# Routing by mask and prefix scan, and a gather inside every preceding expert, in a two-block network with 16 experts

## The chip, the cores and the metric

The kernel runs on one core of one Trainium2 chip. The metric is the device time of one execution in microseconds (us). Before the change it is 2507.76 us, the median of three runs (2507.17 to 2512.72).

## What is computed

Two blocks, one after the other, on 256 tokens of width 1024 (with 16 meta tokens ahead in the first block: T = 272). The first block is a convolution branch and a bidirectional state-space scan, merged, projected and added to the residual h; then comes the part that the change touches:

```python
def expert_choice_ffn(xn, w_router, w_gate, w_up, w_down):
    cap = CAPACITY_FACTOR * T // N_EXPERTS          # 34
    aff = softmax(einsum('btd,de->bte', xn, w_router), axis=-1)
    top_aff, top_idx = top_k(swapaxes(aff, 1, 2), cap)
    xg = xn[bi, top_idx]
    hg = einsum('becd,edf->becf', xg, w_gate)
    hu = einsum('becd,edf->becf', xg, w_up)
    y = einsum('becf,efd->becd', silu(hg) * hu, w_down)
    y = y * top_aff[..., None]
    return zeros_like(xn).at[bi, top_idx].add(y)
```

xn is rms_norm(h). Each of 16 experts picks its own 34 tokens, runs a gated FFN of width 2048 on them, and adds the result back, weighted by the affinity. All is float32. The order of the 34 tokens within an expert doesn't matter to the sum. The second block (gated linear attention, window attention, a product-key layer) follows and isn't touched.

## The kernel before

**Layout.** h lies transposed: 1024 features as 8 tiles of 128 partitions, tokens along the free axis. Each engine has its own written program per stage; semaphores order them.

**End of the mixer.** TensorE computes the eight output tiles with `proj` (line 586), and after tile m calls `norm_sums(m - 2)` (line 767): for three groups of tokens, the sums of squares (weights `s.conf`, one moving column) and the router's products (weights `s.h`, 16 moving columns), each float32 matmul being two records of the trace. The sums of the last three tiles stand behind the last projection. DVE adds the residual (line 579), ACT squares (line 954). SP meanwhile issues the first expert weights (lines 319 to 340).

**Expert weights.** Each expert has 12 units of 2 MB: eight of gate and up rows in turn, four of down. A ring of six slots takes them; the first three units of expert 0 go to rooms of their own (`first_rooms`) that are not filled again. SP (lines 1049 to 1054) waits for unit i to be used and then issues the load six units on. So nine units are loaded before the routing ends.

**Routing** (`experts`, line 1004). ACT and DVE make softmax affinities; TensorE turns the tokens from features-major to tokens-major (line 1127; `s.h` against diagonal matrices of the norm's gain), all six halves, and then the affinities (line 1132) to 16 rows of 272. ACT scales the turned tokens by the norm and rounds them (`tok_hi`, line 1191); DVE makes the rest (`tok_lo`, line 1206). DVE finds the top 34 of each row in five rounds of MAX8, FIND_INDEX8 and MATCH_REPLACE8 (lines 1240 to 1243). From the index lists a spread matrix is made (line 1245), a matmul with ones repeats it over the partitions (line 1140), and a comparison with the row number gives the 0/1 matrix `onehot` for all slots (line 1212). TensorE gathers for eight experts at once, features by slots, as `tok_hi` and `tok_lo` times `onehot` (line 1079, 272 moving columns), ACT copies them out (`picked`, line 1169). `gather(1)` for experts 8 to 15 runs between expert 0 and expert 1.

**An expert.** POOL copies its 34 columns to `tokens` (line 1059). TensorE does 64 products with the tokens as weights (line 1091: 128x34 weights, 512 moving columns, two column groups of the array in turn); ACT silu (1176), DVE the product (1269), and then for each half of the hidden width: four transposes (1099), a DVE copy (1273), 16 down products (1108). ACT copies y (1179); TensorE scatters: eight matmuls of y with `spread` (1118), each added to h by DVE (1277), over two PSUM banks. `spread` (34 rows in each half of the partitions, 272 tokens, the affinity where the token is the slot's) is one DVE instruction per expert from `list_t` (1263), made at the end of the expert before.

What sets the order of TensorE, cut to the loop of an expert:

```python
def expert(e):
    pe.wait_ge(picked, e + 1)
    for u in range(8): ...            # products, L1091
    for c in range(2):
        pe.wait_ge(hidden, 2 * e + c + 1 + FIRST)
        ...                           # four transposes, L1099
        pe.wait_ge(turned_out, 2 * e + c + 1)
        ...                           # down products, L1108
    pe.wait_ge(y_out, e + 1)
    pe.wait_ge(onehot, e + 1)
    for m in range(KT): ...           # scatter, L1118
```

Of the kernel before, what the change touches and what calls it, by code (L numbers as in the profile page):

```python
# [15 lines left out]
P = 128  # L16
# [7 lines left out]
D = 1024  # L24
# [28 lines left out]
FIRST = 1  # L53
# [169 lines left out]
def mixer(nc, s):  # L223
# [60 lines left out]
    with nc.Block() as block:  # L284
# [23 lines left out]
        def _(sp):  # L308
# [5 lines left out]
            for i in range(len(w.units)):  # L314
# [6 lines left out]
                if i in before:  # L321

                    sp.wait_ge(pair_done, PAIRS)
                    s.load_expert_unit(sp, 0, AHEAD + before[i])
# [5 lines left out]
            for u in range(AHEAD - 1):  # L330
                for part in range(2):
                    s.load_expert_unit(sp, 0, u, part)
            s.load_expert_unit(sp, 0, AHEAD - 1, 0)
            s.load_expert_unit(sp, 0, AHEAD)
            sp.wait_ge(tiled, pos["out", 3] + 1)
            s.load_expert_unit(sp, 0, AHEAD + 4)
            sp.wait_ge(tiled, pos["out", 7] + 1)
            s.load_expert_unit(sp, 0, AHEAD - 1, 1)
            s.load_expert_unit(sp, 0, AHEAD + 1)
            s.load_expert_unit(sp, 0, AHEAD + 5)  # L340
# [244 lines left out]
        def _(pe):  # L585
            def proj(t):
# [19 lines left out]
                else:  # L606
# [5 lines left out]
                    for n in parts_of[t]:  # L612
# [8 lines left out]
                        last.then_inc(hi_used, 1)  # L621
                        pe.wait_ge(w_lo, n + 1)
# [144 lines left out]
            def norm_sums(m):  # L767
                pe.wait_ge(hsq, m + 1)
                if m == 0:
                    pe.wait_ge(ystd, 1)  # L770
                    pe.wait_ge(router, 1)

                for j, (t0, n) in enumerate(TT):
                    pe.matmul(ps[0:n, 7, j:j + 1], s.conf[:, m, t0:t0 + n], s.ones[:, 0:1], start=m == 0 and j == 0,
                              stop=False, skip_group_check=True)
                for j, (t0, n) in enumerate(TT):
                    pe.matmul(ps[0:n, 7, EXPERTS * (j + 1):EXPERTS * (j + 2)], s.h[:, m, t0:t0 + n], s.w_router[:, m, :],
                              start=False, stop=m == KT - 1, skip_group_check=True)
# [186 lines left out]
SMALL_ROOMS = 1056  # L965
UNITS = 12


def expert_place(e, u):

    q = (u + EXPERT_RING - AHEAD) % EXPERT_RING
    return q, UNITS // EXPERT_RING * e + (u - AHEAD) // EXPERT_RING + 1


def expert_rows(s, e, u):

    if isinstance(e, int) and UNITS * e + u < AHEAD:
        return s.first_rows[u]
    q = expert_place(0, u)[0]
# [4 lines left out]
def expert_loader(s):  # L984
# [8 lines left out]
    def load(sp, e, u, part=None):  # L993
        if UNITS * e + u < AHEAD:
            sp.dma_start(s.first_rows[u][part], source(e, u)[:, part, :]).then_inc(s.first_in[u], 16)
# [8 lines left out]
def experts(nc, s):  # L1004
# [6 lines left out]
    names = ("rstd3", "std3", "shifted", "exp", "aff", "turned", "lists", "lists_t", "index_rows", "onehot", "tok", "tok_zero",  # L1011
             "tok_out", "tok_rest", "gathered", "gathered_out", "cleared")
    (rstd3, std3, shifted, exped, aff_ready, turned_aff, lists, lists_t, index_rows, onehot_ready, tok, tok_zero,
     tok_out, tok_rest, gathered, gathered_out, cleared) = (s.sem(f"route_{k}") for k in names)
    names = ("picked", "products", "silu", "hidden", "turned", "turned_out", "down", "y", "onehot", "scattered", "added")
    (picked, products, silu, hidden, turned, turned_out, down, y_out, onehot, scattered, added) = (
        s.sem(f"expert_{k}") for k in names)
    w, load, ps, aff, exp = s.w, s.load_expert_unit, s.ps, s.aff, s.aff_exp
    HALF_SLOTS = SLOTS // 2
# [6 lines left out]
    def tok_part(part, j, q):  # L1026
        return part[0:TT[j][1], j, 512 * q:512 * q + 512]

    def arrived(pe, e, u):
        if isinstance(e, int) and UNITS * e + u < AHEAD:  # L1030
            pe.wait_ge(s.first_in[u], 32)
        else:
            q, count = expert_place(0, u)
            pe.wait_ge(s.expert_in[q], 16 * (UNITS // EXPERT_RING) * e + 16 * count)
        return expert_rows(s, e, u)
# [8 lines left out]
    with nc.Block() as block:  # L1044

        @block.sync
        def _(sp):
            for i in range(AHEAD, UNITS * EXPERTS - EXPERT_RING):
                freed(sp, i // UNITS, i % UNITS)
                load(sp, (i + EXPERT_RING) // UNITS, (i + EXPERT_RING) % UNITS)  # L1050
# [5 lines left out]
        def _(pool):  # L1056
            def pick(half, e):
                pool.wait_ge(products, 8 * e + 8 * EXPERTS // 2 * half + FIRST)
                pool.tensor_copy(s.tokens[:, :, :], s.picked[half][:, :, bass.ds(e * CAP, CAP)]).then_inc(picked, 1)

            for part in (s.tok_hi, s.tok_lo):
                pool.memset(part[:, 2, :].bitcast(F32), 0.0).then_inc(tok_zero, 1)
            pool.wait_ge(gathered_out, KT)
            with pool.Fori(0, EXPERTS // 2) as e:
                pick(0, e)
            pool.wait_ge(gathered_out, 2 * KT)
            with pool.Fori(0, EXPERTS // 2) as e:
                pick(1, e)

        @block.tensor  # L1070
        def _(pe):
            def gather(half):
                for m in range(KT):
                    i = KT * half + m
                    if i >= 2:
                        pe.wait_ge(gathered_out, i - 1)
                    for j in range(3):
                        for part in (s.tok_hi, s.tok_lo):
                            last = pe.matmul(ps[:, 6 + i % 2, 0:HALF_SLOTS], part[:, j, P * m:P * m + P],
                                             s.onehot[:, j, HALF_SLOTS * half:HALF_SLOTS * (half + 1)],  # L1080
                                             start=j == 0 and part is s.tok_hi, stop=j == 2 and part is s.tok_lo)
                    last.then_inc(gathered, 1)

            def expert(e):
                pe.wait_ge(picked, e + 1)
                for u in range(8):
                    rows = arrived(pe, e, u)
                    for k in range(2):
# [6 lines left out]
                    last.then_inc(products, 1)  # L1095
                for c in range(2):
# [17 lines left out]
                pe.wait_ge(onehot, e + 1)  # L1114
# [5 lines left out]

            for sem in (products, turned, down, scattered):
                pe.sem_inc(sem, FIRST)
            for j, (t0, n) in enumerate(TT):
                for q in range(2):
                    for r in range(4):
                        k = 4 * q + r
                        last = pe.matmul(by_block(ps[0:n, 2 * j + q, :], r), s.h[:, k, t0:t0 + n],
                                         s.diag[k].rearrange("q (p k) -> q k p", k=2), start=True, stop=True)
                    last.then_inc(tok, 1)
# [5 lines left out]

            pe.wait_ge(lists, 1)
            pe.wait_ge(tok_out, 2)
            pe.wait_ge(tok_rest, 2)
            for half in range(2):
                pe.matmul(ps[:, half, 0:HALF_SLOTS], s.ones[0:EXPERTS, :], s.apart[:, HALF_SLOTS * half:HALF_SLOTS * (half + 1)],  # L1140
# [1385 lines left out]
```

## Time and profile before

| | |
|---|---|
| median of three runs | 2507.76 us |
| the runs | 2507.17, 2507.76, 2512.72 us |
| span of the profiled execution | 2505.9 us |
| busy in the span: PE, DVE, ACT, POOL | 94%, 48%, 29%, 1% |
| bytes moved, mean rate | 677.08 MB, 270 GB/s |

The profiled execution's own time is not listed beside the runs; its span is what its record gives, from the first to the last instruction, and the median of the runs is 1.9 us above it. PE is the matmul queue of TensorE and PEld its weight loads. A PE time in a timeline row is from the first start to the last modelled end of the merged records; where records follow each other closely, the starts of neighbouring rows tell the rate. PEclk is the granted TensorE clock as a share of full speed.

### The profile page before, as it was taken

The page shows a single profiled execution, that of the slowest core. Times are in us where ns is not written, and L with a number is a line of the kernel's source. Part 1 is how long each engine was busy: PE and PEld are TensorE (multiplying, and loading weights), DVE is VectorE, ACT ScalarE, POOL GpSimd, SP SyncE. Part 2 cuts the span into 40 slices and gives each one's busy share as a digit, 9 for nine tenths or more (in the row PEclk, how much of TensorE's full clock was granted, in tenths as well). Part 3 has the DMA queues.
Part 4 walks back from the last instruction along what each step waited for, and adds up shares of the span by engine and source line. Part 5 has one row for each costly group of instructions (what it writes and reads, how often), then busy time and mean ns, then how long its engine had stood idle before and what let it go on. Part 6 is the DMA issues. An engine that isn't in the chain of part 4 may idle for free. (4 is left out here: it accounts for less than half of the span.)

```text
span 2505.9 us, 35019 instructions
## 1 busy us (share of the span) xinstructions
PE 2356.9 (94%) x14241; PEld 1581.3 (63%) x14241; DVE 1202.2 (48%) x2445; ACT 722.3 (29%) x1268; POOL 22.5 (1%) x38
## 2 busy tenths in 40 slices
PE   8999999989998988989898979999999999999998
PEld 6786778963222222222222237889999999888887
DVE  5677876631111111111111125248887776788887
ACT  2145556420000000000000012324454444455554
POOL 1000000000000000000000000000000000000000
PEclk9999999989999999999999989899999999999999
DMA  5375555738999999999999982314775555877775
GB/s 169 112 220 185 175 170 171 254 158 362 428 428 427 428 428 428 428 427 428 428 428 428 428 326 69 123 62 152 225 227 180 173 176 180 252 241 242 241 241 163
DMA packets 205424, 677.08 MB, mean 270 GB/s; under 512 B 15072, under 2 KB 137200, under 8 KB 180336
## 3 DMA queue, kind: packets, MB, share of 16 engines
q1 hardware_dynamic: 205296, 675.30, 72.9%
q8 instruction: 90, 1.47, 0.2%
q14 instruction: 38, 0.31, 0.0%
HBM read 657.40 MB, written 17.83 MB: 269 GB/s over the span
## 5 line engine op out<-in xcount | busy, mean ns | idle before, releaser
L1091 PE MATMUL ps<-ring,tokens 128*34 128x512 f32 x1248 | 273.6, 593 | 16.4 <-DMA ring<-in_w_up 16.4
L1269 DVE TENSOR_TENSOR first_room<-first_room,ps 98x512 f32<-98x512 f32 x32 | 21.8, 682 | 503.6 <-PE ps L1091 503.6
L2126 PE MATMUL ps<-m_hi,row_hi 128*128 128x256 f32 x1024 | 256.5, 288 | 0.8 <-ACT peer_s L2192 0.8
L2126 PE MATMUL ps<-m_lo,row_hi 128*128 128x256 f32 x1024 | 250.7, 283 | 0.0
L605 PE MATMUL ps<-u,ring 128*128 128x272 f32 x1024 | 244.7, 395 | 3.0 <-DVE ring L423 2.9
L605 PEld LDWEIGHTS ps<-u,ring 128*128 128x128 f32 x1024 | 191.5, 190 | 46.1 <-issue 7.2
L1091 PE MATMUL ps<-extra_early,tokens 128*34 128x512 f32 x752 | 198.6, 680 | 11.6 <-DMA extra_early<-in_w_gate 9.8
L1091 PEld LDWEIGHTS ps<-ring,tokens 128*34 128x34 f32 x1248 | 72.2, 112 | 215.0 <-issue 186.4
L1108 PE MATMUL ps<-ring,first_room 128*34 128x512 f32 x768 | 181.1, 619 | 25.2 <-DVE first_room L1273 22.9
L2126 PEld LDWEIGHTS ps<-m_hi,row_hi 128*128 128x128 f32 x1024 | 195.7, 191 | 1.6 <-issue 1.0
L2126 PEld LDWEIGHTS ps<-m_lo,row_hi 128*128 128x128 f32 x1024 | 196.1, 191 | 0.0
L1958 DVE TENSOR_TENSOR row_lo<-u,row_hi 128x1024 fp32r<-128x1024 f32 x128 | 156.6, 1224 | 54.6 <-ACT row_hi L2213 54.2
L1958 DVE TENSOR_TENSOR row_lo<-rows,row_hi 128x1024 fp32r<-128x1024 f32 x128 | 156.6, 1224 | 52.0 <-ACT row_hi L2213 51.3
L1176 ACT ACTIVATE first_room<-ps 98x512 f32<-98x512 f32 x32 | 17.3, 594 | 518.3 <-PE ps L1091 518.3
L2213 ACT ACTIVATE row_hi<-u 128x1024 fp32r<-128x1024 f32 x128 | 135.3, 1057 | 86.6 <-PE ps L2139 86.6
L2213 ACT ACTIVATE row_hi<-rows 128x1024 fp32r<-128x1024 f32 x128 | 135.2, 1057 | 84.7 <-PE ps L2139 84.7
L1277 DVE TENSOR_TENSOR h<-h,ps 128x272 f32<-128x272 f32 x128 | 56.0, 438 | 190.2 <-PE ps L1118 189.3
L1091 PEld LDWEIGHTS ps<-extra_early,tokens 128*34 128x34 f32 x752 | 47.4, 126 | 156.3 <-issue 129.6
L2129 PE MATMUL ps<-m_hi,row_lo 128*128 128x256 f32 x1024 | 143.7, 283 | 0.0
L2139 PE MATMUL ps<-row_hi,act_lo 128*128 128x512 f32 x512 | 137.0, 389 | 0.5 <-DVE act_lo L1992 0.5
L2139 PE MATMUL ps<-row_hi,act_hi 128*128 128x512 f32 x512 | 136.9, 389 | 0.0
L2139 PE MATMUL ps<-row_lo,act_hi 128*128 128x512 f32 x512 | 136.8, 389 | 0.0
(425 smaller groups left out, 3232.0 us busy)
## 6 DMA issues: line engine op xcount, KB each, us to landing
ring<-in_w_down SPq DMA_DIRECT2D x48, 2048.0 KB, 21.6
ring<-in_w_up SPq DMA_DIRECT2D x47, 2048.0 KB, 24.5
extra_early<-in_w_gate SPq DMA_DIRECT2D x31, 2048.0 KB, 18.2
ring<-in_w_gate SPq DMA_DIRECT2D x31, 2048.0 KB, 24.5
ring<-in_w_in SPq DMA_DIRECT2D x36, 1024.0 KB, 5.5
extra_early<-in_w_up SPq DMA_DIRECT2D x16, 2048.0 KB, 25.7
extra_early<-in_w_down SPq DMA_DIRECT2D x16, 2048.0 KB, 25.2
rows<-in_peer_u SPq DMA_DIRECT2D x64, 512.0 KB, 3.8
```

Of the source, the lines that this page charges most:

```text
L605: last = pe.matmul(bank[:, 0:T], wt[:, k, c:c + P], s.u[:, k, :], start=k == 0, stop=k == KT - 1)
L1091: last = pe.matmul(s.ps[HALF * j:HALF * j + CAP, 2 * c + u % 2, :], s.tokens[:, 2 * (u // 2) + k, :], rows[k][:, 1024 * c + 512 * j:1024 * ...
L1108: last = pe.matmul(s.ps[HALF * half:HALF * half + CAP, 5, :], s.hidden_t[:, c, q, HALF * j:HALF * j + CAP], wd[q // 2][:, 1024 * (q % 2) + ...
L1176: act.activation(s.silu[:, c, :], s.ps[0:PAIR, 2 * c, :], ACT.Silu).then_inc(silu, 1)
L1269: dve.tensor_tensor(s.hidden[:, c, :], s.silu[:, c, :], s.ps[0:PAIR, 2 * c + 1, :], ALU.mult)\
L1277: dve.tensor_tensor(s.h[:, m, :], s.h[:, m, :], s.ps[:, 6 + m % 2, 0:T], ALU.add).then_inc(added, 1)
L1958: dve.tensor_tensor(s.row_lo[:, i % 2, :], s.rows[i % ROWS], s.row_hi[:, i % 2, :].bitcast(F32), ALU.subtract).then_inc(lo_done, 1)
L2126: pe.matmul(out, hi[:, P * k:P * k + P], m[:, k, :], start=k == 0 and m is s.m2_hi, stop=False)
L2129: last = pe.matmul(out, lo[:, P * k:P * k + P], s.m2_hi[:, k, :], start=False, stop=k == KT - 1)
L2139: last = pe.matmul(s.ps[:, 4 + 2 * q + half, :], a[:, j % 2, P * q:P * q + P], v[:, 512 * half:512 * half + 512], start=j == 0 and sem is ...
L2213: act.activation(s.row_hi[:, i % 2, :], s.rows[i % ROWS], ACT.Copy).then_inc(hi_done, 1)
```

## The change

- At the end of the mixer, the router's half of `norm_sums` comes first, and the sums of tile m - 1 come after tile m (those of tile 6 inside the last projection, ahead of its lower part), so that only tile 7's are left behind it.
- The ring is filled from unit 0; units 6 to 8 of expert 0 go to the separate rooms.
- The turned tokens are kept once, in float32 (`s.tok`), and not as two parts; three halves are turned ahead of the affinities, three behind.
- FIND_INDEX8 is gone. After five rounds the picked entries of `work` are -1; an is_equal gives the mask `picked`, a prefix scan the rank, their product `place_at`: the slot number 1 to 34 of a picked token, else 0. It is turned by three matmuls to tokens by experts (`place_t`), and comparisons with 1 to 34 give the 0/1 columns.
- Each expert's tokens are gathered by 24 float32 matmuls of 34 moving columns, inside the expert before it, between its products and its transposes. POOL copies the 0/1 columns (`hot`) ahead; ACT copies the result to `tokens` in two halves.
- `spread` is made in each expert from two matmuls that repeat the expert's row of `place_at` and of the affinities over 98 partitions (weights `pick_row`, written by POOL), a comparison and a multiplication on DVE.

The core of the diff:

```diff
-            for m in range(KT):
-                proj(pos["out", m])
-                if m >= 2:
-                    norm_sums(m - 2)
-            norm_sums(KT - 2)
+            for m in range(KT - 1):
+                proj(pos["out", m])
+                if m >= 1:
+                    norm_sums(m - 1)
+            proj(pos["out", KT - 1], before_lower=lambda: norm_sums(KT - 2))
             norm_sums(KT - 1)
...
+            ringed = [(e, u) for e in range(EXPERTS) for u in range(UNITS) if not in_room(e, u)]
+            for i in range(len(ringed) - EXPERT_RING):
+                freed(sp, *ringed[i])
+                load(sp, *ringed[i + EXPERT_RING])
...
+            def mark_row(e):
+                pool.wait_ge(rows_out, e)
+                pool.tensor_copy(s.pick_row[:, :], s.ident[0:EXPERTS, bass.ds(e, 1)].to_broadcast([EXPERTS, PAIR]))\
+                    .then_inc(pick_row, 1)
+
+            def mark_tokens(e):
+                pool.wait_ge(gathered, 2 * e)
+                pool.tensor_copy(s.hot[:, :, :], s.onehot[:, :, bass.ds(e * CAP, CAP)]).then_inc(hot, 1)
...
+            def gather(e):
+
+                pe.wait_ge(hot, e + 1)
+                for half in range(2):
+                    for m in range(4):
+                        for j in range(3):
+                            last = pe.matmul(gathered_at(half)[:, CAP * m:CAP * m + CAP],
+                                             s.tok[:, j, P * (4 * half + m):P * (4 * half + m) + P], s.hot[:, j, :],
+                                             start=j == 0, stop=j == 2)
                     last.then_inc(gathered, 1)
...
-            def expert(e):
-                pe.wait_ge(picked, e + 1)
+            def expert(e, gather_next=True):
                 for u in range(8):
                     rows = arrived(pe, e, u)
+                    if u % 4 == 0:
+                        pe.wait_ge(tokens_in, 2 * e + u // 4 + 1)
...
                     last.then_inc(products, 1)
+                pe.wait_ge(added, KT * e + FIRST)
+                if gather_next:
+                    gather(e + 1)
+                pe.wait_ge(pick_row, e + 1)
+                pe.wait_ge(tokens_in, 2 * e + (4 if gather_next else 2))
+                for bank, values in ((6, s.place_at), (7, s.aff_t)):
+                    last = pe.matmul(s.ps[0:PAIR, bank, 0:T], s.pick_row[:, :], values[:, :], start=True, stop=True)
+                last.then_inc(rows_out, 1)
                 for c in range(2):
                     pe.wait_ge(hidden, 2 * e + c + 1 + FIRST)
...
+            for i in range(3):
+                turn_tokens(i)
             pe.wait_ge(aff_ready, 1)
...
+            for i in range(3, 6):
+                turn_tokens(i)
+            pe.wait_ge(placed, 1)
+            for j, (t0, n) in enumerate(TT):
+                last = pe.matmul(place_cols[0:n, j, :], s.place_at[:, t0:t0 + n], s.ident[0:EXPERTS, 0:EXPERTS],
+                                 is_transpose=True, start=True, stop=True)
+            last.then_inc(place_t, 1)
+            pe.wait_ge(tok_zero, 1)
+            pe.wait_ge(tok_out, 6)
             gather(0)
             pe.wait_ge(cleared, 1)
...
+            def store_tokens(e):
+                for half in range(2):
+                    act.wait_ge(gathered, 2 * e + half + 1)
+                    act.activation(s.tokens[:, 4 * half:4 * half + 4, :], gathered_at(half).rearrange("p (m c) -> p m c", m=4),
+                                   ACT.Copy).then_inc(tokens_in, 1)
...
+            def expert(e):
+                for c in range(2):
+                    dve.wait_ge(silu, 2 * e + c + 1)
+                    dve.wait_ge(products, 8 * e + 8 + FIRST)
+                    dve.wait_ge(turned, 2 * e + FIRST)
+                    dve.tensor_tensor(s.hidden[:, c, :], s.silu[:, c, :], s.ps[0:PAIR, 2 * c + 1, :], ALU.mult)\
+                       .then_inc(hidden, 1)
+                dve.wait_ge(rows_out, e + 1)
+                dve.wait_ge(scattered, KT * e + FIRST)
+                dve.tensor_scalar(s.spread[:, :], s.ps[0:PAIR, 6, 0:T], s.slot_at[0:PAIR, 0:1], None, ALU.is_equal).then_inc(matched, 1)
+                dve.wait_ge(matched, e + 1)
+                dve.tensor_tensor(s.spread[:, :], s.spread[:, :], s.ps[0:PAIR, 7, 0:T], ALU.mult).then_inc(spread, 1)
...
-            link(dve.tensor_copy(s.work[:, :], ps[0:EXPERTS, 6, 0:T]))
+            values = ps[0:EXPERTS, 6, 0:T]
             for r in range(ROUNDS):
                 at = slice(8 * r, 8 * r + 8)
-                link(dve.max(s.top[:, at], s.work[:, :]))
-                link(dve.max_index(s.top_at[:, at], s.top[:, at], s.work[:, :]))
-                if r + 1 < ROUNDS:
-                    link(dve.match_replace(s.work[:, :], s.top[:, at], s.work[:, :], -1.0))
+                link(dve.max(s.top[:, at], values))
+                if r == ROUNDS - 1:
+                    link(dve.memset(s.top[:, CAP:8 * ROUNDS], -1.0))
+                link(dve.match_replace(s.work[:, :], s.top[:, at], values, -1.0))
+                values = s.work[:, :]
+            link(dve.tensor_scalar(s.picked[:, :], s.work[:, :], -1.0, None, ALU.is_equal))
+            link(dve.tensor_tensor_scan(s.rank[:, :], s.picked[:, :], s.picked[:, :], 0.0, ALU.add, ALU.max))
+            dve.tensor_tensor(s.place_at[:, :], s.rank[:, :], s.picked[:, :], ALU.mult).then_inc(placed, 1)
```

## Rows read from the trace of the kernel before

**Rows 1.** Windows: stretch, us, busy of PE, PEld, DVE, ACT, POOL, PEclk, DMA share, GB/s.

```profile
618.00:1470.00 852.00, 765.40 (x3176) 226.47 (x3174) 91.11 (x186) 24.61 (x44) 5.79 (x14) 0.93 1.01 428
594.00:618.00 24.00, 21.71 (x102) 13.02 (x100) 3.91 (x9) 3.78 (x9) 0.00 (x0) 0.86 0.76 308
```

**Rows 2.** Timeline of POOL: start, duration, line, what, and the idle time before.

```profile
694.71 0.41 POOL L1059 COPY tokens<-picked 128x272 f32 x1 [54.02 <-PE ps L1091]
...
1104.35 0.41 POOL L1059 COPY tokens<-picked 128x272 f32 x1 [58.42 <-PE ps L1091]
```

**Rows 3.** Timeline of PE in a late expert.

```profile
1100.54 3.63 PE L1091 MATMUL ps<-ring,tokens 128*34 128x512 f32 x16 [1.28 <-DMA ring<-in_w_up]
```

**Rows 4.** Timeline of PE around the second expert, with every weight in place.

```profile
670.32 13.90 PE L1091 MATMUL ps<-ring,tokens 128*34 128x512 f32 x64
...
695.31 0.72 PE L1099 MATMUL ps<-ident,first_room 98*128 98x98 f32 x4 [0.79 <-DVE first_room L1269]
696.78 7.06 PE L1108 MATMUL ps<-ring,first_room 128*34 128x512 f32 x32 [0.75 <-DVE first_room L1273]
...
719.02 5.89 PE L1091 MATMUL ps<-extra_early,tokens 128*34 128x512 f32 x16
```

**Rows 5.** Timeline of PE: first products of expert 0 and of expert 1.

```profile
550.97 3.63 PE L1091 MATMUL ps<-first_room,tokens 128*34 128x512 f32 x16 [1.28 <-issue]
...
612.43 3.63 PE L1091 MATMUL ps<-extra_early,tokens 128*34 128x512 f32 x16 [0.85 <-ACT picked L1169]
```

**Rows 6.** Timeline of PE: norm sums, turned tokens, turned affinities.

```profile
518.26 0.74 PE L774 MATMUL ps<-ones,conf 128*128 128x1 f32 x6
518.93 0.76 PE L777 MATMUL ps<-w_router,h 128*128 128x16 f32 x6
...
521.95 2.65 PE L1127 MATMUL ps<-lists_t,h 128*128 128x128 f32 x12 [0.90 <-PEq L284]
...
525.25 1.72 PE L1127 MATMUL ps<-lists_t,h 128*128 128x128 f32 x12
...
529.27 0.49 PE L1132 MATMUL ps<-ident,aff 128*16 128x128 f32 x3
```

**Rows 7.** Timeline of DVE: one of the five rounds, and what stands around them.

```profile
529.80 0.43 DVE L1237 COPY std<-ps 16x272 f32<-16x272 f32 x1 [0.87 <-PE ps L1132]
530.26 0.43 DVE L1240 MAX8 top<-std 16x8 f32<-16x272 f32 x1
530.73 0.08 DVE L1241 MATCH_VALUE_LOAD top_at<-top,std 16x8 f32 x1
...
531.26 0.08 DVE L1243 MATCH_VALUE_LOAD std<-top,std 16x8 f32 x1
...
531.79 0.43 DVE L1240 MAX8 top<-std 16x8 f32<-16x272 f32 x1
```

**Rows 8.** Groups by line, DVE: count, busy us, mean ns, idle before.

```profile
L1731 DVE TENSOR_TENSOR_SCAN b<-one_row,cum 128x256 f32<-128x256 f32 x2 | 1.3, 680 | 0.0
```

**Rows 9.** Timeline of PE at the experts' end, and PE busy, PEclk, DMA, GB/s there.

```profile
1477.81 5.93 PE L1118 MATMUL ps<-spread,first_room 34*128 34x272 f32 x16 [0.94 <-ACT first_room L1179]
1487.33 6.99 PE L1467 MATMUL ps<-wn,sq 128*128 128x2 f32 x32 [3.59 <-DVE g L1690]
...
1488.00:1489.00 1.00, 1.00 (x6) 0.50 1.05 387
```

**Rows 10.** Timeline of PE: the index rows, at half clock.

```profile
538.34 2.18 PE L1140 MATMUL ps<-lists_t,ones 16*128 16x272 f32 x4 [8.58 <-DVE lists_t L1245]
```

**Rows 11.** Timeline of PE in the second block, and windows of it (columns as rows 1).

```profile
1558.85 14.09 PE L1413 MATMUL ps<-dq,keys 64*16 64x16 f32 x192
...
1559.00:1563.00 4.00, 4.00 (x82) 3.72 (x76) 3.71 (x7) 0.15 (x2) 0.00 (x0) 1.00 0.79 233
1564.00:1572.00 8.00, 8.00 (x95) 7.59 (x94) 5.04 (x20) 6.34 (x29) 0.00 (x0) 0.50 1.05 387
```

**Rows 12.** Timeline of PE: down products of a late expert.

```profile
1047.58 8.76 PE L1108 MATMUL ps<-ring,first_room 128*34 128x512 f32 x32 [0.75 <-DVE first_room L1273]
```

More of the change, by code:

```diff
@@ L1004, in experts @@
 def experts(nc, s):
[L1011 to L1015, printed above, removed]
@@ L1016, in experts @@
-    (picked, products, silu, hidden, turned, turned_out, down, y_out, onehot, scattered, added) = (
-        s.sem(f"expert_{k}") for k in names)
+    names = ("rstd3", "std3", "shifted", "exp", "aff", "turned", "aff_t", "placed", "place_t", "marked", "tok", "tok_zero",
+             "tok_out", "slot_at")
+    (rstd3, std3, shifted, exped, aff_ready, turned_aff, aff_t_out, placed, place_t, marked, tok, tok_zero,
+     tok_out, slot_at) = (s.sem(f"route_{k}") for k in names)
+    names = ("hot", "gathered", "tokens", "pick_row", "rows", "products", "silu", "hidden", "turned", "turned_out", "down", "y",
+             "matched", "spread", "scattered", "added", "cleared")
@@ L1018, in experts, with gathered_at @@
+    (hot, gathered, tokens_in, pick_row, rows_out, products, silu, hidden, turned, turned_out, down, y_out,
+     matched, spread, scattered, added, cleared) = (s.sem(f"expert_{k}") for k in names)
     w, load, ps, aff, exp = s.w, s.load_expert_unit, s.ps, s.aff, s.aff_exp
-    HALF_SLOTS = SLOTS // 2
+    place_cols = ps[:, 7, 0:3 * EXPERTS].rearrange("p (j e) -> p j e", j=3)
     def by_block(bank, r):
         return bank.rearrange("t (b k s p) -> t b k s p", b=2, k=2, s=2)[:, r // 2, :, r % 2, :]
-    def tok_part(part, j, q):
-        return part[0:TT[j][1], j, 512 * q:512 * q + 512]
+    def gathered_at(half):
+        return s.ps[:, 6 + half, T:T + 4 * CAP]
@@ L1056, in _ @@
         def _(pool):
[L1057 to L1065, printed above, removed]
@@ L1070, in _ @@
+            pool.memset(s.tok[:, 2, :], 0.0).then_inc(tok_zero, 1)
+            pool.tensor_copy(s.pick_row[:, :], s.ident[0:EXPERTS, 0:1].to_broadcast([EXPERTS, PAIR])).then_inc(pick_row, 1)
+            pool.wait_ge(marked, 2)
+            mark_tokens(1)
+            with pool.Fori(1, EXPERTS - 1) as e:
+                mark_row(e)
+                mark_tokens(e + 1)
+            mark_row(EXPERTS - 1)
         @block.tensor
         def _(pe):
[L1072 to L1081, printed above, removed]
+            def gather(e):
[6 more added lines that the diff above has]
+                                             start=j == 0, stop=j == 2)
@@ new lines, in _ @@
+            for j in range(3):
+                last = dve.tensor_tensor(s.onehot[:, j, CAP:SLOTS].rearrange("p (e c) -> p e c", c=CAP),
+                                         s.place_t[:, j, 1:EXPERTS].unsqueeze(2).to_broadcast([P, EXPERTS - 1, CAP]),
+                                         s.iota[:, 1:CAP + 1].unsqueeze(1).to_broadcast([P, EXPERTS - 1, CAP]), ALU.is_equal)
+            last.then_inc(marked, 2)
+            dve.wait_ge(slot_at, 1)
+            expert(0)
+            with dve.Fori(1, EXPERTS) as e:
+                expert(e)
```

238 lines of the change are left out of this document (93 added, 145 removed).

## The prediction

> **What bounds the kernel now.** I read the stretch of the experts first (from about 521 us to 1484 us), in windows, since the change lies there. Over 852 us in the middle of it the DMA share is 1.01 and 428 GB/s flow; before that, around the second gathering, it is 0.76 [rows 1]. So the stage looks bound by the expert weights. The question for a change that adds TensorE work is how much room TensorE has. POOL copies each expert's tokens when the last product of the expert before is done, so the distance of two copies is the time of one expert: 58.42 + 0.41 = 58.83 us late in the stage, but 54.02 + 0.41 = 54.43 us for the second expert, while the ring was full [rows 2]. The first figure is the DMA's (12 units of 2 MB, 4.90 us each), the second is TensorE's own: with all weights there it has no wait for DMA in it, while late experts show waits of about 1.3 us before single units [rows 3]. **TensorE has 58.83 - 54.43 = 4.4 us of room per expert, and no more.**
>
> Its own 54.43 us, from the second expert's timeline [rows 4]: four units of products in 13.9 us at full clock (3.43 us from start to start), then a chain of 0.79 us idle until DVE has the hidden row, 0.72 transposing, 0.75 idle until DVE has copied it, 7.06 of down products, the same again shorter, 0.94 for y, and the scatter. The first unit behind the scatter takes 5.89 us instead of 3.63 [rows 5], because the clock has fallen to half in the scatter.
>
> **The head, up to the first product of expert 0.** Before, that is at 550.97 us [rows 5].
> - Norm sums. One output tile's sums are 12 records in 1.37 us: the two groups of six start 0.67 us apart [rows 6]. Before, three tiles' sums (4.1 us) follow the last projection. After, two of them go ahead of its end (TensorE is dense there, so that costs 2.7 us), then the residual add (0.6 us with its semaphores), the router half and the squares' half (1.4 us) follow: 4.7 us, so +0.7 us. The expert loads are only reordered: nine units before the routing, as now; SP's queue behind them stays the same, and they are in by 532 us, with no one waiting for them.
> - Tokens turned. 48 records run ahead of the turning of the affinities, which starts at 529.27 [rows 6]. Now 24 of them do: 3.1 us at half clock at 0.206 us each (first 16 in 3.3 us), then nine at 0.14. The affinities would be ready (the Exp table is loaded ahead) before that. DVE's first MAX8 comes at about 527.55 instead of the copy at 529.80: -2.25 us.
> - Top 34. A round is 1.53 us before (530.26 to 531.79), of which FIND_INDEX8 with its load is 0.53; without it 1.00 [rows 7]. Five rounds, a memset of 0.2, and no copy: they end at 532.75. Then the mask (0.45), the scan (0.76: 256 columns took 0.68 [rows 8]) and a multiply (0.47): 534.4. Transposes 0.55, hot and place_t 0.55: 535.5. The index rows, the marks and list_t are gone from the path; marks and memset now run beside gather(0), 6 us of DVE beside more than that of TensorE.
> - gather(0): 24 float32 matmuls, 48 records, each with 128x128 weights and 34 moving columns. This operation is not in the trace. Its nearest rows have weights of that size and 16 or 1 moving columns: 0.11 us per record at full clock [rows 6], and 0.218 at half (32 records in 6.99 us, clock 0.50 [rows 9]). Those weights, not the columns, set the rate, and I see no row of that size below 0.11. TensorE has been idle for 5 us and stands at half clock, and in rows 9 such records did not raise it in 7 us. So 48 x 0.218 = 10.5 us, and the first product comes at **546.1 us, 4.9 us sooner**. Bounds: 5.3 us (full clock) to 10.5.
> The Trainium skill ("TensorE: Matmul & The Clock Gate", section "LDWEIGHTS (loading the stationary operand)") gives a weight load as its columns over 1.2, without a term for the clock. By that, gather(0) would take 5.1 us and the first product would come 5 us earlier still, 2579 us in all. Rows 9 speak against it, and the sum goes by them.
>
> **Each expert.** Every expert but the last now gathers for its successor between its products and its transposes, and TensorE's order is fixed: nothing else can go there. Per expert, at full clock:
> - gather: 48 x 0.11 = +5.3 us;
> - wait for ACT to copy its second half (tokens_in stands ahead of the row matmuls): between 0.4 and the 0.85 us of the like wait at the second gathering [rows 5]; 128x136 is half as wide, +0.6;
> - two row matmuls of 16x98 weights and 272 columns: four such records took 2.18 us at half clock [rows 10], so 1.1 less a tail, +0.95;
> - DVE: is_equal and multiply (2 x 0.43 as the old spread) start when the rows are out and end 0.25 us too late for the first copy of the transposes: +0.25. Behind them wait that copy and so the down products;
> - the 0.79 us wait for the hidden row is covered by the gather: -0.79.
> Free: POOL's two copies and ACT's silu (beside the gather), the spread taken from the tail. Sum: +6.3 us, 54.43 + 6.3 = **60.7 us. That is over 58.83: TensorE becomes the bound.** The ring then holds, since the loads need only 58.83.
>
> **The clock comes on top.** A stretch of weight loads with few moving columns (16), in which TensorE was never idle, begins at 1558.85 at full clock; the clock falls between 1563 and 1564 and stays at half to the end [rows 11]. I take it that the gather, the wait, the rows over 16 partitions and the transposes, 9 us together, do the same in each expert. Price: the end of the gather at half clock 0.7, rows and transposes 0.8, and the first down units 1.7, as in a late expert where waits of that length brought it down and the 32 records took 8.76 us [rows 12] instead of 7.06 [rows 4]. Sum 3.2 us: **63.9 us per expert.** Bounds: 0 to 8.5.
> Section "Why this matters for your kernels" of the same page of the Trainium skill warns of idle gaps between bursts of matmuls only; by it a busy gather would keep 2.4 GHz and 60.7 us would stand. Rows 11 disagree for 16 columns; no row has 34.
>
> **Sum.** Expert 15 gathers nothing: 54.43 + 0.95 + 0.25 - 0.79 and 0.8 of clock = 55.6. The last scatter ends at 546.1 + 15 x 63.9 + 55.6 = 1560.2 us, against 1477.81 + 5.93 = 1483.74 [rows 9]: +76.5 us. What follows waits for the sum of squares and not for its weights, and is unchanged. The span goes from 2505.9 to 2582.4; the median of the runs is 1.9 us above the span, so 2584.3 us.
>
> **Rivals.**
> 1. The clock holds in the gather. For: 34 columns are more than 16, and all 128 rows are used. 546.1 + 15 x 60.7 + 55.0 = 1511.6, +27.9: 2536 us. Chance 0.25.
> 2. Faster: the gather's weight loads run under the tail of the products and the row matmuls under the gather, so that it adds less than the 4.4 us of room (the point that decides). Then the DMA stays the bound and starts earlier: first load at 550.6, 183 x 4.90 = 897 us, one hole of 10 us in expert 0 (six ring loads are used up before a seventh slot is free, because units 6 to 8 sit in rooms that aren't refilled), and 10.5 us from the last weights to the end of the scatter: 1469 us, 2493 us in all. Against: 0.11 us a record was measured with TensorE full, so the overlap is in it. Chance 0.05.
> 3. The clock stays low longer: all of the gather (5.3 more) and 2.1 in the down part: 69.2 us an expert, +157: 2665 us. Chance 0.06.
> Between 2 and 1, nearly cancelling: 0.02. The forecast has 0.62.
>
> **How the numbers follow.** About 0.2% (5 us) is what a measurement of this kernel can tell from no change. The range takes in rival 1 and, upwards, a clock price of 5.1 instead of 3.2 us (15 x 1.9 = 28): 2530 to 2612. Faster 0.05, same 0.02, slower 0.93.
>
> **What would show it.** The time between scatters near 64 us with no wait for DMA before products; GB/s near 428 x 58.83/63.9 = 394; 48 gather records in 5.3 to 6.5 us between products and transposes; granted clock 0.5 behind them; MAX8 at 1.00 us a round; first product near 546. It would be wrong if the gather takes under 3 us, if the distance of experts is 58.8 (the DMA still bounds), or if the clock is 1.00 through the gather and the down products.

## The result, and the profile after

The changed kernel takes 2586.11 us (median of four runs, 2584.93 to 2586.93) against 2508.73 us for the kernel before in the same comparison: a ratio of 1.0309, 95% interval 1.0294 to 1.0323. Its profiled execution has a span of 2584.3 us. The forecast was 2584.

First its page: the busy time of the engines, the granted clock in 40 slices (tenths), and the two groups of products.

```profile
PE 2490.2 (96%) x14974; PEld 1680.4 (65%) x14974; DVE 1203.7 (47%) x2445; ACT 725.9 (28%) x1285; POOL 22.3 (1%) x52
...
PEclk9999999988888888888888898899999999999999
...
L1111 PE MATMUL ps<-ring,tokens 128*34 128x512 f32 x1264 | 277.9, 594 | 0.0
...
L1111 PE MATMUL ps<-extra_early,tokens 128*34 128x512 f32 x752 | 197.2, 681 | 0.0
```

The idle time before the products is 0.0 in both groups: no unit of weights is waited for any more, where before single units were [rows 3]. The windows of the experts say the same from the side of the transfers (columns: us, busy of PE, PEld, DVE, ACT, POOL, PEclk, DMA share, GB/s):

```profile
600.00:1540.00 940.00, 899.53 (x3924) 328.87 (x3922) 100.92 (x209) 33.19 (x73) 6.44 (x27) 0.87 0.94 392
```

392 GB/s against 428 [rows 1]: the transfers no longer bound the stage, TensorE does. The timeline of POOL gives the distance of two experts (start, duration, line, and the idle time before):

```profile
584.70 0.26 POOL L1074 COPY pick_row<-ident 16x98 f32 x1 [37.54 <-PE ps L1122]
...
1096.60 0.26 POOL L1074 COPY pick_row<-ident 16x98 f32 x1 [62.95 <-PE ps L1122]
1160.34 0.26 POOL L1074 COPY pick_row<-ident 16x98 f32 x1 [63.27 <-PE ps L1122]
```

The fifteenth such copy starts at 1480.44, so an expert takes (1480.44 - 584.70) / 14 = 63.98 us, against 58.83 [rows 2]. Where they go is in the timeline of PE in one expert:

```profile
1084.02 3.60 PE L1111 MATMUL ps<-ring,tokens 128*34 128x512 f32 x16
1087.55 6.39 PE L1098 MATMUL ps<-hot,tok 128*128 128x34 f32 x48
1094.31 1.22 PE L1122 MATMUL ps<-place_at,pick_row 16*98 16x272 f32 x2 [0.37 <-ACT tokens L1190]
1095.33 1.11 PE L1122 MATMUL ps<-aff_t,pick_row 16*98 16x272 f32 x2
1096.37 0.93 PE L1127 MATMUL ps<-ident,first_room 98*128 98x98 f32 x4
1098.07 9.14 PE L1136 MATMUL ps<-ring,first_room 128*34 128x512 f32 x32 [0.77 <-DVE first_room L1240]
```

Nine microseconds (1087.55 to 1096.37) stand between the products and the transposes, and the first 32 down records take 9.14 us instead of 7.06 [rows 4]. The windows of the same stretch show the clock (us, PE busy, PEclk, DMA share, GB/s):

```profile
1090.00:1092.00 2.00, 2.00 (x20) 1.00 0.94 401
1092.00:1094.00 2.00, 1.94 (x10) 0.51 0.98 418
1094.00:1098.00 4.00, 2.99 (x8) 0.50 1.04 442
...
1102.00:1104.00 2.00, 2.00 (x10) 0.93 1.06 451
```

TensorE was busy without a pause up to 1092, and its clock fell from the 2.4 to the 1.2 GHz level inside the gather, before any wait. It came back at about 1102, four microseconds into the down products. The moment differs: in 7 of the gathers of experts 1 to 14 the clock held to the last records, as at 1216.33, where the gather takes 5.55 us and the granted clock is 0.87 from 1221 to 1222 and 0.50 in the microsecond after. The 32 down records then take 8.4 or 10.0 us.

The head, in the timeline of PE:

```profile
521.11 0.74 PE L780 MATMUL ps<-ones,conf 128*128 128x1 f32 x6
522.75 2.90 PE L1154 MATMUL ps<-lists_t,h 128*128 128x128 f32 x12 [0.90 <-PEq L284]
...
526.30 1.91 PE L1154 MATMUL ps<-lists_t,h 128*128 128x128 f32 x8
528.00 0.75 PE L1164 MATMUL ps<-ident,aff 128*16 128x128 f32 x3
...
536.32 10.43 PE L1098 MATMUL ps<-hot,tok 128*128 128x34 f32 x48 [0.56 <-DVE place_t L1280]
546.67 8.36 PE L1111 MATMUL ps<-ring,tokens 128*34 128x512 f32 x32
```

And in that of DVE, first round, mask and scan:

```profile
528.79 0.44 DVE L1268 MAX8 top<-ps 16x8 f32<-16x272 f32 x1 [4.00 <-PE ps L1164]
...
529.79 0.43 DVE L1268 MAX8 top<-replaced 16x8 f32<-16x272 f32 x1
...
533.88 0.29 DVE L1273 TENSOR_SCALAR picked<-replaced 16x272 f32<-16x272 f32 x1
534.21 0.71 DVE L1274 TENSOR_TENSOR_SCAN rank<-picked 16x272 f32<-16x272 f32 x1
```

The head is 4.3 us shorter (first product at 546.67 instead of 550.97 [rows 5]), a round takes 1.00 us instead of 1.53 [rows 7], and expert 0 starts sooner. The fifteen gathers take that back many times over.

### The profile page after: what moved, and what is told of

Read it like the earlier page. It is cut to its first block and busy times, and to the rows that moved or that the text cites. A ratio compares the mean times of both kernels' runs of the same rounds, so it can differ in the third digit from the quotient of the medians.

```text
span 2584.3 us, 36562 instructions
## 1 busy us (share of the span) xinstructions
PE 2490.2 (96%) x14974; PEld 1680.4 (65%) x14974; DVE 1203.7 (47%) x2445; ACT 725.9 (28%) x1285; POOL 22.3 (1%) x52
## 5 line engine op out<-in xcount | busy, mean ns | idle before, releaser
L1136 PE MATMUL ps<-ring,first_room 128*34 128x512 f32 x752 | 200.3, 690 | 22.4 <-DVE first_room L1240 22.4
L1136 PEld LDWEIGHTS ps<-ring,first_room 128*34 128x34 f32 x752 | 47.0, 127 | 154.5 <-issue 125.1
```

The costliest lines, as they stand in the source:

```text
L1136: last = pe.matmul(s.ps[HALF * half:HALF * half + CAP, 5, :], s.hidden_t[:, c, q, HALF * j:HALF * j + CAP], wd[q // 2][:, 1024 * (q % 2) + ...
```

## The experiments

The theory is the forecast's: TensorE has 4.4 us of room per expert, the gather's records overrun it, and the clock adds about 3.2 us. The rivals are that the clock is no part of it, and that the room is not what it looks like. The kernel before took 2507.6 to 2508.3 us in the comparisons below; "distance" is that of two experts late in the stage, from POOL's copies.

**e1_no_gather: the changed kernel without the gathers in the loop** (all experts work on the tokens of expert 0; gathering for experts 1 to 15 is left out, with the copies by POOL and ACT that belong to it).

```diff
-            expert(0)
+            expert(0, gather_next=False)
             with pe.Fori(1, EXPERTS - 1) as e:
-                expert(e)
+                expert(e, gather_next=False)
...
```

> Leaves out the gathers inside the experts; every expert works on the tokens of expert 0, all else as after the change. TensorE-bound theory: own time of an expert falls to 54.9 us (as expert 15 has it), under the 58.83 of the loads, so the DMA bounds again and the earlier start shows: about 2492 us, experts 58.8 us apart. Rival (the new order of the loads, with rooms in the middle of expert 0, starves the ring): the time stays above 2510. Rival (the row matmuls, the DVE steps and the waits are the cost, not the gather): stays above 2550.

Measured 2499.82 us, ratio 0.9964 (0.9950 to 0.9979). In the timeline of POOL the third expert's copy:

```profile
685.60 0.26 POOL L1074 COPY pick_row<-ident 16x98 f32 x1 [54.23 <-PE ps L1118]
```

TensorE's own time is 54.23 + 0.26 = 54.49 us with the row matmuls in it, and late in the stage the distance is 58.84: the loads' again. So the gathers, with their copies and what they do to the clock, turn a small gain into the loss, 2586.11 - 2499.82 = 86 us. The time is 8 us above what was expected. The windows of the first experts (us, PE busy, PEclk, DMA share, GB/s):

```profile
550.00:560.00 10.00, 10.00 (x50) 1.00 0.78 305
...
580.00:590.00 10.00, 9.34 (x46) 1.00 0.60 230
...
600.00:610.00 10.00, 10.00 (x41) 0.82 0.52 190
```

The second rival of the forecast, whose case this is, had the loads start at 550.6, one hole of 10 us in expert 0 and the end of the last scatter at 1469. Here they start at about 552.2 (0.78 of the slice), there are two holes, of 4.0 and 4.8 us, and the scatter ends at 1473.3. So the holes together are not larger than forecast. Of the 4.3 us, 1.6 are the later start, and the smaller holes give 1.2 back. The other 3.9 are not explained: that 4.90 us is rounded (58.83 / 12 = 4.903) makes 0.5 of them over 183 units. The rest of the 8 us lies in the runs: the profiled execution, at 2497.03, was the fastest of the five, and their median is 2.8 us longer.

**e2_dose12 and e3_dose24: the kernel before plus 12 or 24 matmuls of the gather's shape per expert**, results unused.

```diff
+                pe.wait_ge(added, KT * e + FIRST)
+                for _ in range(24):
+                    pe.matmul(s.ps[:, 6, T:T + CAP], s.picked[0][:, 0, 0:P], s.picked[0][:, 0, P:P + CAP], start=True, stop=True)
```

> The kernel before with 12 extra float32 matmuls (24 records, 128x128 weights, 34 columns, result unused) per expert between products and transposes, and nothing else. TensorE-bound theory: 2.65 us at full clock, 0.8 of it under the wait for the hidden row, at most 1.7 for the clock: 56.3 to 58.0 us an expert, inside the room of 4.4, so no change: 2507 to 2513 us. Rival (any added TensorE time lengthens the chain, as the loads wait for the slots that TensorE frees): +1.9 us x 16 = 30, so 2538.

> The same with 24 extra matmuls (48 records) per expert. TensorE-bound theory: 54.4 + 5.3 - 0.8 = 58.9 us and 1.5 to 3.2 us for the clock, 60.5 to 62 us an expert: 2530 to 2560 us. If the clock holds through such matmuls: 58.9 us an expert, about 2515. Rival (any added time counts): 2585 or more.

Twelve: 2513.24 us, ratio 1.0017 (1.0008 to 1.0027), at the upper end of what was expected; distance 58.84, unchanged. Twenty-four: 2563.06 us (one run), 3 us above the expected range; distance 61.4, inside it. Half the dose costs 5 us and the whole 55: the room ends between the two. Some 4 of the 5 us lie in the first two distances (64.20 and 55.84 us, in the kernel before 61.47 and 54.44), where the loads are not yet the bound and every added record counts. The timeline of PE in e3, and windows of it (us, PE busy, PEclk, DMA share, GB/s):

```profile
1077.57 5.67 PE L1098 MATMUL ps<-picked 128*128 128x34 f32 x48
...
1084.69 9.51 PE L1111 MATMUL ps<-ring,first_room 128*34 128x512 f32 x32 [0.75 <-DVE first_room L1276]
1094.14 0.72 PE L1102 MATMUL ps<-ident,first_room 98*128 98x98 f32 x4
```

```profile
1077.00:1083.00 6.00, 6.00 (x52) 0.99 1.01 431
1085.00:1089.00 4.00, 4.00 (x12) 0.50 1.01 430
```

**e9_dense11: the same TensorE time in dense matmuls**, 11 of 272 columns in the place of the 24 of 34.

```diff
+                pe.wait_ge(added, KT * e + FIRST)
+                for _ in range(11):
+                    pe.matmul(s.ps[:, 6, 0:T], s.picked[0][:, 0, 0:P], s.picked[0][:, 1, 0:T], start=True, stop=True)
```

> The kernel before plus 11 float32 matmuls of 272 columns per expert between products and transposes, results unused: 22 records of 0.239 us are 5.26 us, the same TensorE time as the 24 matmuls of 34 columns in e3_dose24 (48 records, 5.3 us), but in dense columns. Theory (narrow matmuls cost their time and besides let TensorE's clock fall, which the expert's own down products then pay): here the clock stays, an expert's own work is 54.4 + 5.3 - 0.8 = 58.9 us, about the loads' 58.8, and the time is 2520 to 2535. Rival (the clock costs nothing, only the added TensorE time counts): the same time as e3, 2563. The granted clock over the added matmuls is 1.00 by the theory.

Measured 2514.75 us, ratio 1.0028 (1.0018 to 1.0038), 5 us below the expected range, because the distance is 58.05 and not 58.9 (why, in the last section). The timeline of PE and one window of it:

```profile
1054.37 5.31 PE L1098 MATMUL ps<-picked 128*128 128x272 f32 x22
...
1060.87 7.06 PE L1111 MATMUL ps<-ring,first_room 128*34 128x512 f32 x32 [0.75 <-DVE first_room L1276]
1067.86 0.72 PE L1102 MATMUL ps<-ident,first_room 98*128 98x98 f32 x4
```

```profile
1060.00:1064.00 4.00, 3.25 (x18) 1.00 0.97 414
```

From 1054 to 1060, over the added matmuls, the granted clock is 1.00 too. This is the cleanest pair of the study. From the start of the added matmuls to the second transposes e3 takes 1094.14 - 1077.57 = 16.57 us and e9 takes 1067.86 - 1054.37 = 13.49: 3.08 us, of which 2.45 is in the down products and the rest in the added matmuls' end and the transposes. Per expert 61.4 - 58.05 = 3.35; the other 0.27 lie in the scatter and the first unit behind it (11.42 us against 11.15). The same busy time costs 7 us in all when dense and 55 when narrow (2514.75 and 2563.06 against 2507.6 and 2508.3). The "clock costs nothing" rival, which wanted 2563 here, is out.

**e4_rows_late: the changed kernel with the row matmuls behind the first transposes**, where DVE copies.

```diff
-                pe.wait_ge(pick_row, e + 1)
-                ...
-                last.then_inc(rows_out, 1)
                 for c in range(2):
...
                     last.then_inc(turned, 1)
+                    if c == 0:
+                        pe.wait_ge(pick_row, e + 1)
+                        ...
+                        last.then_inc(rows_out, 1)
...
```

DVE makes the spread behind its first copy in turn.

> After the change, with the two row matmuls moved behind the first four transposes, so that they run while TensorE waits for DVE's copy, and DVE making the spread after that copy. Theory: the wait for ACT's token copy (0.37), the later copy (0.25) and most of the row matmuls leave the path: about 1.4 us an expert, 62.6 us, 2565 us. Rival (TensorE isn't the bound, or the clock takes it back in a longer stretch at half): within 5 us of 2586.

Measured 2562.6 us, ratio 1.0216 (1.0198 to 1.0233), distance 62.5. The place of two small matmuls is worth 23.5 us, 1.5 us per expert. In its trace the wait for ACT is gone and the rows run while DVE copies the transposes: from the start of the gather to the first down product it takes 8.26 us in the expert at 1078, where the changed kernel takes 9.67 to 10.52. How the 1.5 us divide between the two was not tried.

**e6_spread_gather: e4, with three of the gather's matmuls behind each unit of products** instead of 24 at the end.

```diff
                     last.then_inc(products, 1)
+                    if gather_next:
+                        ...
+                        gather_block(u)
                 pe.wait_ge(added, KT * e + FIRST)
-                if gather_next:
-                    gather(e + 1)
```

> After the change with the row matmuls behind the first transposes, and the gather's 24 matmuls spread over the eight units of products, three behind each, where dense matmuls stand around them. Clock theory: the same 48 records at 0.11 us, but no fall of the clock before the down products: 54.4 + 5.3 + about 0.4 = 60.1 us an expert, 2525 to 2530 us. Rival (the price of the gather is the records alone and the clock costs nothing): as e4, about 2565.

Measured 2545.95 us, ratio 1.0154 (1.0137 to 1.0171), 16 us above the expected range, distance 61.35 instead of 60.1. The timeline of PE and the windows of it:

```profile
1042.94 0.86 PE L1106 MATMUL ps<-hot,tok 128*128 128x34 f32 x6
1043.72 3.63 PE L1120 MATMUL ps<-ring,tokens 128*34 128x512 f32 x16
1047.28 0.86 PE L1106 MATMUL ps<-hot,tok 128*128 128x34 f32 x6
...
1076.02 7.06 PE L1149 MATMUL ps<-ring,first_room 128*34 128x512 f32 x32
```

```profile
1042.00:1074.00 32.00, 32.00 (x166) 1.00 0.99 406
1074.00:1078.00 4.00, 3.90 (x20) 1.00 0.99 422
```

The clock holds, as expected, and the down products are back at 7.06. But two units now start 4.34 us apart where 3.43 is a unit's own [rows 4]: each group costs 0.91 us and not 6 x 0.11 = 0.66, so the eight cost 7.3 us instead of 5.3. Those 2 us are more than the 1.25 by which the distance missed, so something else came out 0.7 us better than the expectation, and what was not looked for. Against e4 (62.5) the count closes: the spread gather saves the clock's 3.2 us and gives back 2.

**e7_pair_spread: e6, but a gather takes the tokens of two experts at once** (68 columns per matmul), in every second expert.

```diff
-                    last = pe.matmul(gathered_at(half)[:, CAP * m:CAP * m + CAP],
-                                     s.tok[:, j, P * u:P * u + P], s.hot[:, j, :],
+                    last = pe.matmul(gathered_at(half)[:, 2 * CAP * m:2 * CAP * m + 2 * CAP],
+                                     s.tok[:, j, P * u:P * u + P], s.hot[:, j, :], start=j == 0, stop=j == 2)
```

> As e6, but gathered for two experts at once (68 columns) in every second expert, and for experts 0 and 1 at the start. Theory: weight loads set the rate, so 68 columns cost what 34 do: 2.7 us an expert on the mean, 57.5 us, under the 58.83 of the loads: the DMA bounds, 2492 us, faster than both kernels. Rival (columns set the rate): 60.1 us an expert, as e6. Rival (uneven experts starve or overfill the ring): 2500 to 2515.

Measured 2500.12 us (seven runs, 2498.00 to 2502.42), ratio 0.9966 (0.9954 to 0.9977): **faster than both kernels**, than the one before by 0.3%. The timeline of PE:

```profile
1070.14 0.89 PE L1097 MATMUL ps<-hot,tok 128*128 128x68 f32 x6
1070.96 3.63 PE L1110 MATMUL ps<-ring,tokens 128*34 128x512 f32 x16
...
1152.25 3.63 PE L1110 MATMUL ps<-ring,tokens 128*34 128x512 f32 x16 [0.25 <-DMA ring<-in_w_up]
```

Twice the columns cost 0.89 us a group instead of 0.86. Experts take 54 to 55 and 61 to 64 us in turn. Up to 1041 us they take 57.7 on average (57.5 was expected), behind that 58.83: the loads' pace, and a wait for DMA is back in front of a unit. The time is 8 us above the expectation and on the edge of its second rival, that uneven experts starve the ring (2500 to 2515). Against starving speaks that from 610 to 1450 us the DMA share is 1.01 at 427 GB/s, as in e1. The loads start at 553.4 (0.66 of the slice below), 1.2 us later than e1's, and the last scatter ends at 1475.66, 2.4 us after e1's. The rest of the miss stays open, as in e1.

**e10_pair_rooms_first: e7 with the old order of the loads** (the rooms hold units 0 to 2 again).

```diff
-FIRST_ROOM = 6
+FIRST_ROOM = 0
...
```

> e7_pair_spread with the load order undone: the rooms that are kept free are the first three units again, as in the kernel before. Theory: the hole in the loads of experts 0 and 1 only moves (it is set by how long TensorE keeps its rooms while the head and two gathers pass), so the time stays within 3 us of e7, 2497 to 2503. Rival (the new order of loads and rooms is itself a gain or a loss): 5 us or more to either side, seen as a wider or narrower hole in the loads between 550 and 610 us.

Measured 2500.92 us, ratio 0.9972 (0.9961 to 0.9983). Windows of e10, and then of e7 (columns as above):

```profile
550.00:560.00 10.00, 10.00 (x50) 1.00 0.00 0
560.00:570.00 10.00, 10.00 (x48) 1.00 0.79 303
```

```profile
550.00:560.00 10.00, 10.00 (x50) 1.00 0.66 251
...
580.00:590.00 10.00, 9.34 (x46) 1.00 0.63 229
...
600.00:610.00 10.00, 10.00 (x39) 0.77 0.60 226
```

The old order leaves 10.0 + 2.1 = 12.1 us without transfers ahead, the new one 3.4 + 3.7 + 4.0 = 11.1 in three pieces. The hole only moves; the new order of the loads is worth nothing that this measurement can tell.

**e11_pair_norms: e7 with the norm sums where the kernel before has them.**

```diff
-            for m in range(KT - 1):
+            for m in range(KT):
...
-                if m >= 1:
-                    norm_sums(m - 1)
-            proj(pos["out", KT - 1], before_lower=lambda: norm_sums(KT - 2))
+                if m >= 2:
+                    norm_sums(m - 2)
+            norm_sums(KT - 2)
```

> e7_pair_spread with the move of the norm sums undone: their matmuls stand where the kernel before has them. Theory: the sums end 0.7 to 0.8 us sooner (the changed kernel ended them at 521.85 us, the kernel before at 521.05), the first product starts 0.7 sooner, and the total moves by that or less, 2499 to 2500, seen in the trace alone. Rival (the move was a gain): up to 2.7 us longer, 2503.

Measured 2501.18 us, ratio 0.9967 (0.9956 to 0.9979). First products at 545.99 us, in e7 at 547.68, in e10, whose sums stand as in e7, at 546.41. Single traces differ by more than the 0.7 us in question, so they leave that open. A gain of 2.7 us from the move is not seen: the seven times of e11 have a mean of 2500.8 us, those of e7 one of 2500.4.

**e5_warm_head and e8_pair_warm: seven matmuls of 272 columns in the idle time before gather(0)**, in the changed kernel and in e7, to have the higher clock there.

```diff
+            for i in range(7):
+                pe.matmul(ps[:, 7, 64:64 + T], s.h[:, i, 0:P], s.h[:, i, :], start=True, stop=True)
             pe.wait_ge(placed, 1)
```

> After the change, with seven float32 matmuls of 272 columns (result unused) in the 3.6 us in which TensorE waits for the top 34. Theory: they keep the clock full, gather(0) takes 48 x 0.11 = 5.3 us instead of 10.4, unless the clock falls inside it; first product near 541.6 instead of 546.7, and 2581 us in all. Rival (the weight loads take 0.22 us a record here for another reason than the clock): no change, 2586.

> e7 with the seven matmuls of e5 ahead of the first gather. Theory: a DMA-bound stage starts 5 us sooner: 2487 us. Rival (the hole in the loads of expert 0 takes it back): 2492.

e5: 2582.02 us, ratio 1.0294 (1.0277 to 1.0311); the timeline of PE, and windows of it:

```profile
536.46 6.52 PE L1098 MATMUL ps<-hot,tok 128*128 128x34 f32 x48 [0.56 <-DVE place_t L1282]
542.91 9.36 PE L1111 MATMUL ps<-ring,tokens 128*34 128x512 f32 x32
```

```profile
539.00:541.00 2.00, 2.00 (x19) 0.94 0.00 0
541.00:543.00 2.00, 2.00 (x12) 0.50 0.00 0
```

The same 48 records take 6.52 us instead of 10.43: all but the last 2 us of the gather ran at the higher clock. Then it fell inside the busy gather, and the first two units took 9.36 us instead of 8.36. The first product came at 542.91 instead of the expected 541.6, and the kernel gains 4.1 us. In e7's frame the same edit brings nothing that can be told (2499.29, ratio 0.9968, 0.9955 to 0.9980), where 2487 was expected. Its trace shows two things. The clock fell earlier, at about 540.1 us, so the gather took 8.29 us and the first product came at 545.94, only 1.7 us before e7's. And the holes in the loads are there as in e7: the DMA share is 0.63 from 580 to 590 us and 0.60 from 600 to 610.

## Why the prediction was right, step by step

- **The room of 4.4 us and the 54.43 us of TensorE's own**: borne out. e1 shows 54.49 with the row matmuls, where the forecast's terms give 54.84; e2's half dose leaves the distance at 58.84, e3's whole one does not. The two doses enclose the 4.4 us, they do not measure it.
- **The head**: 546.67 instead of 546.1. The norm sums end 0.8 us later than before (+0.7 forecast). The first MAX8 came at 528.79, 1.24 us later than forecast: the step "nine at 0.14" failed, since the turned tokens stayed at the lower clock (0.213 us a record in the eight at 526.30, and the turning of the affinities too took 0.79 us to DVE instead of 0.53). When the clock comes back there is not the kernel's doing alone: it was back at about 528.9 us in this trace, 6 us after the turning began, and at 527.1 in that of e5, which is the same up to there, 2.8 us after it began; e5's eight records took 1.07 us instead of 1.91. The memset (0.06 instead of 0.2), the mask (0.29 instead of 0.45) and the turning of the slots gave some back. A round (1.00) and the scan (0.71 against 0.76) were right.
- **gather(0)**: 10.43 us against 10.5. The window from 537 to 546 shows a granted clock of 0.50. An estimate from the formula of the Trainium skill ("TensorE: Matmul & The Clock Gate", section "LDWEIGHTS (loading the stationary operand)") is 5.1 us; the measurement decides, and e5's 6.52 us, mostly at the higher clock, shows that the clock belongs in that price.
- **The gather in an expert**: 5.55 to 6.39 us, 5.8 on average, against 5.3 + 0.7 = 6.0; right.
- **The wait for ACT**: 0.37 instead of 0.6 us, just under its lower bound of 0.4.
- **The rows**: 2.06 us from 1094.31 to 1096.37, at the lower clock. The forecast had 0.95 and half of 0.8, 1.35 in all; this took up what the ACT wait left, and 0.5 more. The 0.25 us for DVE's spread do not show there: the wait before the down products is 0.77 against 0.75 [rows 4]. In expert 15, where rows and transposes run at full clock, it is 1.02.
- **The clock's price**: 3.2 us forecast as an extrapolation from 16 columns [rows 11] to 34. e3 against e9 gives 3.35. The split was less good: the 32 down records took 8.42 to 10.04 us, 9.4 on average, so 2.3 over 7.06 and not 1.7, while the lower clock at the end of the gather cost 0.3 and not 0.7 (5.8 us on average against 5.55 where the clock held). In the expert shown the fall came at 1092, two microseconds before the gather's end. Section "Why this matters for your kernels" of the same page of the Trainium skill warns of idle gaps; in that expert there was none before the fall, so the rule alone would have given rival 1.
- **The sum**: 63.98 us per expert against 63.9, and 54.91 for expert 15 against 55.6, since without a gather its clock stayed up. The last scatter ends at 1561.86 against 1560.2. Part of that agreement is luck: errors of 0.2 to 0.7 us offset one another. From the last product to the second transposes an expert takes 19.3 us on average, 10.0 more than the 9.26 of the second expert before, where the forecast has 9.5 more; the wait for y (0.78 us instead of 0.94) and the scatter with the first unit behind it (11.2 to 11.3 us instead of 11.6) give that back.
- **Rival 1** (the clock holds, 2536) fell: the clock did not hold. e6, where it does, has another order and other costs and takes 2546. **Rival 2** had the right mechanism and the wrong side of its threshold: when gather and clock together fit the room (e7), the DMA is the bound again and the kernel faster, at 2500 and not its 2493. **Rival 3** fell: at most the last 2 us of the gather ran at the lower clock (from 1092 to 1094), not all of it. Its 69.2 us is 63.9 + 5.3; the 2.1 us for the down part that it names besides are not in that sum.

What stays open: what in a matmul keeps the clock up. Narrow ones of 34 columns alone, and dense ones of 272 over 128 rows, were compared, nothing between.

## What to carry to other kernels

Before adding work beside a transfer bound, find TensorE's own time of a period from one in which everything was loaded: the difference to the transfers' time is all that is free, and the price of what goes beyond it is paid in every period. Price narrow matmuls (few moving columns, full weights) by their weight load, and add what the following dense work loses at the lower clock; serve two consumers with one matmul, since here 68 columns took hardly longer than 34 (0.89 against 0.86 us a group), and spread such groups among dense ones.

## What the hardware showed that was not expected

- A small group of narrow matmuls between dense ones costs about 0.25 us beyond its records (0.91 against 0.66 us, e6).
- TensorE's clock falls during uninterrupted narrow work: at about 1092 in the changed kernel, in e5 at about 541, in e3 at about 1083, as the added matmuls end. In half of the changed kernel's experts it falls only at the end of the gather (1221.7) or in the short wait behind it (1286.6). Over the dense filler of e9, of equal length, it stayed up.
- Work below the room is not free where the transfers aren't yet the bound: 12 matmuls per expert cost 5 us in e2, most of it in the first experts.
- The distance of experts in e9, 58.05 us, is below the loads' 58.83 and the expected 58.9, so that TensorE caught up on stored weights until a DMA wait of 0.44 us came back at 1399. The clock falls in its scatter too, but earlier (its granted clock is 0.83 from 1078 to 1080 and 0.50 to 1086, with the scatter starting at 1077.16; in the kernel before 0.95 from 715 to 717 and 0.50 behind that, with the scatter starting at 713.16), and lies over less of the next products: their first unit takes 4.89 us instead of 5.89 [rows 4], the scatter 6.50 instead of 5.93, together 0.4 us less. Another 0.3 is that the stretch from the added matmuls to the second transposes takes 13.49 us and not the 13.8 that were expected. After the wait at 1399 the scatter and the first unit take 6.89 and 6.03. Where a low stretch falls moves by microseconds with what ran before it, and can be worth about a microsecond per period.
